# Opening of a state-space scan after a delta-rule stage, and one weight load moved past a stage of 32x32 matmuls

## The reference, cut to what matters

```
def hybrid_layer(h_lat, h_ctx, ...):
    u_l = rms_norm(h_lat, pre_w) * (1 + scale_l[:, None]) + shift_l[:, None]
    u_c = rms_norm(h_ctx, pre_w) * (1 + scale_c) + shift_c
    z_l, xbc_l, dt_l, qkv_l, b_l, a_l = _split_proj(u_l @ w_in)
    z_c, xbc_c, dt_c, qkv_c, b_c, a_c = _split_proj(u_c @ w_in)
    xbc_l = jax.nn.silu(conv_latent(xbc_l, conv_ssd_w) + conv_ssd_b)
    xbc_c = jax.nn.silu(centred_dwconv(xbc_c, conv_ssd_w) + conv_ssd_b)
    qkv_l = jax.nn.silu(conv_latent(qkv_l, conv_gdn_w))
    ssd_c, ssd_l = ssd_mixer(xbc_c, dt_c, xbc_l, dt_l, ssd_a_log, ssd_dt_bias, ssd_d)
    gdn_c, gdn_l = gdn_mixer(qkv_c, b_c, a_c, qkv_l, b_l, a_l, gdn_a_log, gdn_dt_bias)
    ...
```

## Time and profile before

| | |
|---|---|
| three runs, median | 3075.4 us (3070.02 to 3076.04) |
| the profiled execution, its own time | 3067.73 us |
| its span, first to last instruction | 3065.9 us |
| mean granted TensorE clock | 0.992 |
| busy: PE, DVE, ACT, POOL | 2995.0, 1852.6, 1332.6, 187.5 us |
| GDN heads, one turn of the head | 57.7 us in most |
| meeting of the engines | at 613.3 us |
| SSD tiles | from there to about 800 us |

### The profile page before, as it was taken

One profiled execution on the slowest core, in us unless ns is written; L12 is line 12 of the kernel. 1 busy time (PEld: TensorE's weight loads), 2 busy tenths in 40 slices (PEclk: granted clock), 3 DMA queues, 4 the chain that ended last, 5 costly groups with the idle time before them and its releaser, 6 DMA issues.

```text
span 3065.9 us, 68257 instructions
## 1 busy us (share of the span) xinstructions
PE 2995.0 (98%) x28670; PEld 2825.0 (92%) x28670; DVE 1852.6 (60%) x2509; ACT 1332.6 (43%) x1729; POOL 187.5 (6%) x287
## 2 busy tenths in 40 slices
PE   6999999989999999999999999999999999999999
PEld 2677777878989999999999999999999999999999
DVE  3666667678886666555555555566665555555554
ACT  3444545444554444444333333444444443333332
POOL 0000000000110000211000000200002110000000
PEclk8999999999999999999999999999999999999999
DMA  9611121223765544555555555554445555555554
GB/s 397 267 71 70 57 98 71 82 98 110 316 250 206 178 170 159 191 193 194 195 194 195 193 192 192 202 196 175 170 163 192 192 193 193 194 194 195 195 193 150
DMA packets 82960, 547.07 MB, mean 178 GB/s; under 512 B 9125, under 2 KB 13365, under 8 KB 18928
## 3 DMA queue, kind: packets, MB, share of 16 engines
q1 hardware_dynamic: 78448, 523.27, 46.9%
q10 hardware_dynamic: 2192, 15.40, 1.3%
q0 software_dynamic: 2160, 6.05, 0.6%
HBM read 540.46 MB, written 7.36 MB: 179 GB/s over the span
## 4 chain that ended last, share of the span: by engine, by line
PE 91%; DVE 4%; ACT 2%; DMA 1%; issue 1%; PEld 0%; PEldq 0%; SPq 0%; POOL 0%; DVEq 0%; ACTq 0%
PE bank L441 28%; PE bank L443 27%; PE bank L442 27%; PE bank L843 1%; PE bank L716 1%; DVE w_lo L425 1%; DMA raw<-stream 1%; PE bank L946 1%; PE bank L752 1%; DVE s_acc L1633 1%; DMA xr<-x_t 0%; DVE g_L L1775 0%; PE bank L1140 0%; PE bank L768 0%; PE bank L929 0%
## 5 line engine op out<-in xcount | busy, mean ns | idle before, releaser
L420 ACT CAST w_hi<-raw 128x2048 fp32r<-128x2048 f32 x447 | 854.4, 1911 | 1236.3 <-PE bank L443 1236.3
L425 DVE TENSOR_TENSOR w_lo<-raw,w_hi 128x2048 fp32r<-128x2048 f32 x447 | 1026.6, 2297 | 548.1 <-ACT w_hi L420 548.0
L441 PE MATMUL bank<-a_lo,w_hi 128*128 128x256 f32 (+1 forms) x3600 | 1069.7, 297 | 6.7 <-DVE w_lo L425 6.1
L442 PE MATMUL bank<-a_hi,w_lo 128*128 128x256 f32 (+1 forms) x3600 | 1043.7, 290 | 0.0
L443 PE MATMUL bank<-a_hi,w_hi 128*128 128x256 f32 (+1 forms) x3600 | 1043.7, 290 | 0.0
L441 PE MATMUL bank<-h_lo,w_hi 128*128 128x256 f32 x3568 | 995.6, 279 | 6.1 <-DVE h_lo L2056 6.1
L442 PE MATMUL bank<-h_hi,w_lo 128*128 128x256 f32 x3568 | 986.4, 276 | 0.0
L443 PE MATMUL bank<-h_hi,w_hi 128*128 128x256 f32 x3568 | 986.1, 276 | 0.0
L441 PEld LDWEIGHTS bank<-a_lo,w_hi 128*128 128x128 f32 x3600 | 679.0, 189 | 30.3 <-DVE w_lo L425 7.9
L443 PEld LDWEIGHTS bank<-a_hi,w_hi 128*128 128x128 f32 x3600 | 678.0, 188 | 17.7
L442 PEld LDWEIGHTS bank<-a_hi,w_lo 128*128 128x128 f32 x3600 | 679.5, 189 | 12.8
(11 more groups left out here) (348 smaller groups left out, 2039.8 us busy)
## 6 DMA issues: line engine op xcount, KB each, us to landing
raw<-stream SPq DMA_DIRECT2D x485, 1024.0 KB, 4.8
gate_raw<-stream ACTq DMA_DIRECT2D x12, 1024.0 KB, 8.2
xr<-x_t SPq DMA_DIRECT2D x4, 1024.0 KB, 16.4
q_raw<-stream SPq DMA_DIRECT2D x8, 512.0 KB, 9.7
x_res<-x_t SPq DMA_DIRECT2D x1, 2048.0 KB, 16.7
bias_table<-bias SPq DMA_DIRECT2D x1, 2048.0 KB, 10.8
bias<-bias_table ACTq DMA_DIRECT2D x1, 2048.0 KB, 9.4
out_t<-x_res SPq DMA_DIRECT2D x4, 512.0 KB, 5.1
```

The costliest lines, as they stand in the source:

```text
L420: act.copy(w_hi[u.slot][:], raw[u.raw][:]).then_inc(hi_ready, 1)
L425: dve.tensor_tensor(w_lo[u.slot][:], raw[u.raw][:], w_hi[u.slot][:], ALU.subtract).then_inc(lo_ready, 1)
L441: pe.matmul(acc, wh, lo[:, k, 0:n], start=(k == first), stop=False)
L442: pe.matmul(acc, wl, hi[:, k, 0:n], start=False, stop=False)
```

## The change

Six edits:

- **POOL**: `s_pad` is cleared ahead of the meeting, when all convolutions of B and C are done (`conv_done` at 3 * HG + 4), and no longer behind the DMA of the bias table.
- **ACT**: the six Silu activations of B and C move ahead of the meeting, with a load of Silu's table ahead of them. They write `s_bt` and `s_ct`.
- **ACT**: `x_padded` asks for Silu's table after its split, so ahead of the wait for the convolution.
- **DVE**: the split of U_SSD + 2 (z of tile 0) moves from inside tile 0 to right behind the convolution of tile 0.
- **DVE**: tiles 0 to 3 are written out instead of looped.
- **SP**: in the GDN stage `late` is 1 for two raw buffers of four. With u the head's first unit, the load of u + 10 waits for the split of u + 7 (level 5) instead of u + 6 (level 2). The number of loads and their order stay.

The diff (blocks of unchanged functions that only move are cut; ACT's `x_padded`, `x_silu` and `z_silu` now stand behind the meeting as before, behind the activations):

```
@@ SP @@
-                        late = int(end == U_BC // RAW and r == U_GDN % RAW)
+                        late = int(end == U_BC // RAW and r in (U_GDN % RAW, (U_GDN + 2) % RAW))
                         sp.wait_ge(lo_ready, i * RAW + (r + late - RAW + 1 - FIRST))
                         load(i * RAW + r, r)
                 if end == U_BC // RAW:
                     for n in range(end * RAW, U_LAST):
-                        late = int(n in (U_BC, U_BC + RAW))
+                        late = int(n in (U_BC, U_BC + 2, U_BC + RAW, U_BC + RAW + 2))
                         sp.wait_ge(lo_ready, n + late - RAW + 1 - FIRST)
                         load(n, n % RAW)
@@ POOL @@
+            pool.wait_ge(S["conv_done"], 3 * HG + 4)
+            pool.memset(s_pad[:], 0.0).then_inc(S["pads_set"], 1)
             leave(pool, 1)
             pool.wait_ge(S["rel_out"], 16)
             pool.dma_start(*repeated(0, TABLE_HEADS)).then_inc(S["bias_table"], 16)
-            pool.memset(s_pad[:], 0.0).then_inc(S["pads_set"], 1)
@@ ACT @@
-            leave(act, 1)
-            act.wait_ge(S["pads_set"], 2)
...
-            x_padded(Unit(U_SSD))
+            act.preload_act_table_set(SILU)
+            act.wait_ge(S["conv_done"], 3 * HG + 4)
             for j in range(4):
                 b = BC_ORDER[j]
                 out = s_bt[:, b * T:(b + 1) * T] if b < 2 else s_ct[:, (b - 2) * L:(b - 1) * L]
...
                 m.then_inc(S["bc_ready"], 1)
+
+            leave(act, 1)
+            act.wait_ge(S["pads_set"], 2)
+
+            def x_padded(u):
...
+                split_act(act, u.ahead(2))
+                act.preload_act_table_set(SILU)
...
+            x_padded(Unit(U_SSD))
             x_silu(0, 0)
@@ DVE @@
             conv_tile(0, 0)
+            split_dve(dve, Unit(U_SSD + 2))
             dve.wait_ge(S["bc_tok"], 1)
...
                     m.then_inc(S["s_pre"], 1)
-                    if more:
+                    if more and not (isinstance(i, int) and i + t == 0):
                         split_dve(dve, u.ahead(2))
...
-                tiles(dve, g, 2 * 11, tile, own)
+                for k in range(4):
+                    tile(*((k // 2, k % 2) if g == 0 else (0, 4 + k)), g * 4 + k < TS - 1)
```

More of the change, by code:

```diff
@@ L49 @@
 LOG_EXP = "natural_log_exp_and_others"
+SILU = "silu_and_others"
 FQ = 4
@@ L1385, in _ @@
                 head(i, i < HG - 1)
+            act.preload_act_table_set(SILU)
+            act.wait_ge(S["conv_done"], 3 * HG + 4)
+            for j in range(4):
+                b = BC_ORDER[j]
+                out = s_bt[:, b * T:(b + 1) * T] if b < 2 else s_ct[:, (b - 2) * L:(b - 1) * L]
+                m = f(d3(out[:, 0:L], ROW), rows4(g_acc[j][:, 0:264]), ACT.Silu, bias=par("bias_ssd", 8 + b))
+                if b < 2:
+                    m = f(out[:, L:T], g_acc[j][:, 264:520], ACT.Silu, bias=par("bias_ssd", 8 + b))
+                m.then_inc(S["bc_ready"], 1)
             leave(act, 1)
@@ L1415, in _ @@
             x_padded(Unit(U_SSD))
[L1416 to L1422, removed]
             x_silu(0, 0)
```

2 lines of the change are left out of this document (1 added, 1 removed).

## The result

| | before | after |
|---|---|---|
| median of six runs each | 3074.86 us (3070.02 to 3077.81) | 3053.1 us (3047.64 to 3058.34) |
| the profiled execution, its own time | 3067.73 us | 3047.64 us |
| its span | 3065.9 us | 3045.5 us |
| mean granted TensorE clock | 0.992 | 0.994 |
| meeting: PE's first matmul behind it | 613.47 us | 604.49 us |

The medians differ by 21.8 us. The ratio on record for these runs is 0.9939, with a 95% interval of 0.9925 to 0.9953; of 3074.86 us that is 18.8 us less, between 14.5 and 23.1. The forecast was 3057.6 us (17.8 less) and a range from 3049.0 to 3067.5; 3053.1 lies in it. The profiled executions differ by 20.1 us.

A forecast was written before the change was run, and what follows sets the result against it. PE, busy for 98% of the span, was taken to bound the kernel, so only its idle or low-clock time counts. 8.8 + 6.9 (opening) + 2.1 = 17.8 us off the median 3075.4 gave 3057.6 us, range 3049 to 3067.5.

The forecast's parts named there:

- The load in the packed levels: GDN heads 0, 2 and 3: PE's instruction fetch waits behind a 1 MB weight load; moving it saves 8.8 us.
- B and C: Opening of the SSD scan: their activations run before the meeting, so DVE's chain starts 1.65 us earlier.
- the split: DVE's split of z's weights leaves the chain in tile 0: 2.2 us, of which 0.2 is given back.
- the loop: Convolution of tile 1 written out instead of looped: 0.4 us less on DVE's chain.
- the table: Silu's table is loaded before the convolution of tile 1 ends: 1.3 us less on the chain.
- The padding: s_pad cleared before the meeting: ACT pads at about 613.5, convolution of tile 0 ends at 618.0 instead of 619.8 us.
- The slow stretch: PE's half-speed clock after the 3.16 us wait for Silu of tile 1: expected to go, 1.7 us.
- the later tiles: PE's waits for Silu in tiles 2 to 4: expected to go through the early table load, 2.1 us.
- Tile 0 up to Silu of tile 1: DVE's chain at the SSD opening: 5.2 us shorter, PE's turn for tile 1 at 638.3 instead of 643.51.
- The fetch is not the cause: Rival on the packed levels: the load does not hold up the fetch, or stops turn up elsewhere; 3066.4 us, chance 0.15.
- The opening keeps a wait: Rival on the SSD opening: PE still idles, the slow stretch stays, 3 to 4 us less gain; 3061 us, chance 0.18.
- Two loads starve PE: Rival on the heads: the paired loads hold up instructions in level 6 and the state steps; 3081 us, chance 0.03.

The follow-up runs named there:

- a1: The kernel before with the SP edit alone (the load of u + 10 waits for the split of level 5); 3057.99 us, ratio 0.9961.
- d1: The kernel before with 32 small products (128 instructions, half a 16 KB block) more near the start of PE's program; 3059.01 us, one run.
- b2: The changed kernel with s_pad cleared behind the meeting again; from the meeting to PE's turn of tile 1 24.64 us, as in the changed kernel.
- b5: The kernel before with DVE's tiles 0 to 3 written out, nothing else; from the meeting to PE's turn of tile 1 29.62 us against 30.04.
- b3: The changed kernel without the request for Silu's table in x_padded; from the meeting to PE's turn of tile 1 25.92 us against 24.64.
- b1: The kernel before with only B and C's activations and Silu's table load ahead of the meeting; meeting to PE's turn of tile 1 28.22 us against 30.04.
- a2: The changed kernel without the SP edit, so the edits on POOL, ACT and DVE alone; 3062.91 us, ratio 0.9966 to the kernel before.
- a3: The kernel before with two loads (u + 8 and u + 9) instead of one issued at the split of level 2; 3076.31 us, one run.
- a4: The kernel before with 64 small products (256 instructions, a whole block) more near the start of PE's program; 3074.83 us, one run.

## Why the prediction was right, and where it was not

- **The load in the packed levels**, 8.8 us: measured 9.0 at the meeting between the profiles, and a1 gives it alone. The cause was right; the packets of q8 and the half block in d1 show it. The reading that only q8's packet and stragglers came after PE had stopped was loose: the packet starts before the stop (in 278.0 to 278.5, PE stops at 278.7) and PE goes on some 2.3 us after it. What I did not see is that three stops are one execution's number; it was two to five elsewhere.
- **B and C** 1.65, the split 2.0, the loop 0.4, the table 1.3: measured 1.82, 1.87, 0.42, 1.28. Sum taken 5.2, measured 5.40. PE's remaining wait, forecast 1.1, is 1.16.
- **The padding** was credited with an earlier convolution of tile 0. That is so on DVE and worth nothing on the path (b2); my sum had not counted it apart, so no term fails.
- **The slow stretch**, 1.7, and **the later tiles**, 2.1: 3.8 forecast, 3.4 measured from tile 1 to tile 7. Three things are wrong inside it. PE waits 0.49 us for the low half of x of the next tile, since the split behind the convolution ends later than Silu: in the last part of "Tile 0 up to Silu of tile 1" I followed Silu alone and not the split next to it. And "in each the table (1.28) stands between convolution and Silu", so that the early table takes the 2.1 us away, was not needed: b5 shows that writing out the loop does it alone, and b3 that it does so without the early table. The slow stretch itself cost 1.5 and not 1.7: from the turn of tile 1 to the state matmuls of tile 7 it is 137.3 us with it (before, b1) and 135.8 without (a1, d1). That the slow stretch goes was right for this execution and is not shown to be the change's doing (b2, a2, b3 have it).
- **Elsewhere**: 2.6 us of the profiles' difference lie behind the changed part, in stretches of half speed that come and go. They are no part of the effect.
- **The rivals.** "The fetch is not the cause" fell with d1, and what spoke for it, five heads with the same load and no stop, has its answer in the packets: there the fetch got in with the load's start. "The opening keeps a wait" is half true: 1.16 and 0.49 are left, but both within the sum. "Two loads starve PE" fell: the heads are at 57.7 us, and a3 shows that a fetch waits behind one load of a pair, so that the price that I worked out was wrong as well. Its figures were too: 2 MB at the pace of rows 5 are about 4.9 us and not 9, and one load 2.5 and not 4.4; in the traces the packets of one load take 3.4 us (head 2 of before) and those of a pair 5.9 (head 2 of after). The change did what it says.
- **The median**: 21.8 us against 17.8. By the profiles the effect at the edits is 17.8, so the terms were sized for this pair. That this equals the forecast's sum to a tenth is in part luck: the errors above (0.2 each on the load and the opening, 0.4 the other way behind it) cancel. Against the medians the forecast is 4.0 us short, which is within the interval of the runs. If the difference is real, the likely term is that of the load: it counted the stops of one execution, 8.8 us, where five profiles lose 13.2 in the mean. How many stops the median execution has was not measured.

## What to carry to other kernels

Where an engine stops in the middle of a dense run of small instructions and nothing is named as the releaser, look at the DMA queues of those 2 us: if a large transfer fills them and one packet of the instruction queue comes at its end, some 2 us before the engine goes on, move the transfer out of the dense stretch. Price a stop with the low clock behind it, and over several executions, since one profile shows only some of the stops. And in a chain that ends a wait, follow all that hang on the same step: here Silu and the split both follow the convolution, and when one was shortened the other was next.

## What the runs showed of the hardware

- A fetch of instructions that meets a 1 MB load waits for it: PE stood still for 1.45 to 2.5 us in groups of 32x32 matmuls in 19 of 40 heads. In these the q8 packet came 2.8 to 3.9 us after the load's first packet, and PE went on 2.2 to 2.5 us after q8's. In the other 21 the fetch got in within 0.3 us of the load's start.
- The phase of the instruction stream matters too. 128 instructions more at the start of the program removed all the stops, though the fetch still came only with the load's end (d1, one execution); 256 more left them where they were (a4, one execution).
- Behind two loads in one go the fetch waits no longer than behind one: 3.1 to 3.9 us (a3).
- A float32 product is counted as two matmuls and two weight loads: 64 products made 128 of each (a4).
- Idle times of PE of the same length do not always lower the clock. After 3.16 us it fell in before and after 3.18 it did not in a1; after 1.16 and 0.49 it fell in b2 and did not in after. Where it fell at these places it was for 3.4 us at 1.2 instead of 2.4 GHz, which cost 1.5 to 1.7; behind the stop in head 2 of a3 it was for 6.8.
- The same five DVE instructions on the same data take 4.48 us in a hardware loop and 3.68 written out, through gaps of 0.15 to 0.50 us that follow the instruction before on the same engine.
